# Softmax stage of a two-layer decoder: the twelve output matmuls of a unit stand together, behind the transposes

## The chip, the cores and the metric

The kernel runs on one core of a Trainium2 chip. The metric is the device time of one execution in microseconds (us). The engines of the core work side by side, each through a queue of its own in order, and wait for each other by semaphores: TensorE (PE, with its weight loads as PEld), VectorE (DVE), ScalarE (ACT), GpSimd (POOL) and SyncE (SP), which issues the loads and stores.

## What is computed

Two layers over 2048 positions of width 1024: first sliding-window attention with a sink per head, then a pooling mixer. The change lies in the attention. Cut to what matters:

```python
scores = jnp.einsum('bnqkgd,bnskd->bnkgqs', qb, kb) * (HEAD_DIM ** -0.5)     # 16 blocks of 128 queries
scores = jnp.where(mask, scores, -jnp.inf)                                    # own block and the one before
m = jnp.maximum(jnp.max(scores, axis=-1, keepdims=True), sink)
p = jnp.exp(scores - m)
denom = jnp.sum(p, axis=-1, keepdims=True) + jnp.exp(sink - m)
o = jnp.einsum('bnkgqs,bnskd->bnqkgd', p / denom, vb)                         # 4 key heads, 16 query heads
x = x + gate * ((o * jax.nn.silu(g)) @ w_out)
```

## The kernel before

Four stages follow each other: `qkv_stage`, `gate_stage`, `attend_stage` (the softmax stage) and `pool_layer`. Results between them go through device memory. Products of float32 are made of three matmuls, high x high, high x low and low x high, so that most data exist as a high and a low part.

`attend_stage` works through 64 units (`UNITS`), one for each block of 128 queries and each key head with its four query heads. Sixteen units (`LAP`) make a block of 512 positions. All engines run the same loop over i, each with its own part of several units, so that the steps of one unit are spread over four iterations. In iteration i stand:

- TensorE: `scores(i)`, eight matmuls of 256 columns (L1232); `p_round(i-1)`, four transposes of the probabilities `pr` into the PSUM tile `tr` (L1240), which wait for `prob_done` of unit i-1; `values(i-2)`, twelve matmuls of 256 columns into `o_ps` (L1256), which wait for the masked probabilities `pt`.
- VectorE: `gated(i-3)`, which multiplies `o_ps` by the gate into `z` (L1168) and waits for `values(i-3)`, done by TensorE in iteration i-1; `divide(i-1)`, a reciprocal (L1152) and a multiply of `pr` (L1154) that gives `prob_done`; `scores(i)`, a predicated copy (L1144) and a maximum (L1148); `z_lo(i-3)` (L1175), the low part of `z`; `residual(c)` in the iteration in which chunk c has ended (L1183); `p_lo(i-1)` (L1160), the low part of the transposed probabilities.
- ScalarE: `z_hi(i-3)`, `previous(i)` (L1091), `p_hi(i-1)` (L1106), which waits for the transposes, the four exponentials of `exps(i)` (L1099), and `square(c)` (L1123).
- GpSimd: four masks, two of the high part `ph` and two of the low part `pl` (L1051), and `add_square(c)` (L1060), one addition of two tiles in SBUF for each chunk but the first of eight.

The output projection of a block of 512 positions (`output`, L1270) is 8 chunks (c) of 128 output channels, each 24 matmuls of 512 columns. The chunks of the first three blocks (c = 0 to 23) are spread over the units of the next block: chunk c begins in iteration `first_slot(c)` and takes two iterations, twelve matmuls in each. That is iterations 19 to 66. The last eight chunks follow behind the loop. A chunk ended before iteration i has its `residual`, `square` and `add_square` in iteration i; these are the odd iterations from 21 on, and the addition on GpSimd falls into the end of the odd iteration or the start of the even one. The order on each queue is the order in which the code is written. The loop of TensorE is the only place that the change touches (L1284 to L1303, the functions as they are called there).

Of the kernel before, what the change touches and what calls it, by code (L numbers as in the profile page):

```python
# [23 lines left out]
def wait(eng, sem, count):  # L24
    if not (isinstance(count, int) and count <= 0):
        eng.wait_ge(sem, count)
# [870 lines left out]
def attend_stage(nc, sems, others, xt_d, sinks_d, qt_d, kt_d, vs_d, sg_d, wo_d, x1t_d, ident, gate0, rstd1, KC, NB, KV, HEADS, HD, D):  # L897
# [13 lines left out]
    with ExitStack() as ctx:  # L911
# [42 lines left out]
        def first_slot(c):  # L954
            return LAP * (c // KC + 1) + BEHIND + HALVES * (c % KC)
# [7 lines left out]
        def place(m):  # L963
            cur, prev = m % 3, (m - 1) % 3
            return min(cur, prev), max(cur, prev), 0 if cur < prev else 1

        with nc.Block() as block:
# [251 lines left out]
            @block.tensor  # L1219
            def _(pe):  # L1220
                def scores(u):
                    m, g = u // KV, u % KV
                    low, high, _ = place(m)
                    if g == 0:
                        pe.wait_ge(q_loaded[m % 2], 16 * (m // 2 + 1))
                        pe.wait_ge(k_loaded[m % 3], 16 * (m // 3 + 1))
                        if m == 0:
                            pe.wait_ge(zero_set, 1)
                    wait(pe, cur_done, u - 1)
                    for h in range(GROUP):  # L1230
                        for part in (HI, LO):
                            last = nc.tensor.matmul(s_ps[:, u % 2, h, :, :], qt[:, m % 2, GROUP * g + h, :],  # L1232
                                                    kt[:, low:high + 1:high - low, g, part, :], start=(part == HI), stop=(part == LO))
                    last.then_inc(s_done, 1)

                def p_round(u):
                    pe.wait_ge(prob_done, u + 1)
                    wait(pe, pl_done, u)
                    for h in range(GROUP):
                        last = nc.tensor.transpose(tr[:, h * P:(h + 1) * P], pr[:, u % 2, h, 0:P], ident[:, :])  # L1240
                    last.then_inc(ptr_done, 1)

                def values(u):
                    m, g = u // KV, u % KV
                    if g == 0:
                        pe.wait_ge(v_loaded[m % 3], 16 * (m // 3 + 1))
                    pe.wait_ge(pt_done, 4 * (u + 1))
                    wait(pe, z_done, u)
                    parts = [(m % 3, (CUR_HI, CUR_LO))] + ([((m - 1) % 3, (PREV_HI, PREV_LO))] if m > 0 else [])
                    i = 0  # L1250
                    for slot, kinds in parts:
                        for v_part, p_part in PRODUCTS:
                            moving = pt[:, u % 2, kinds[p_part], :].rearrange("p (a b t) -> p a b t", a=2, b=2)
                            for parity in (0, 1):
                                v = vs[:, slot, g, v_part, HD - parity * HD:HD - parity * HD + 2 * HD]
                                last = nc.tensor.matmul(o_ps[:, 0:2 * P], v, moving[:, :, parity, :],  # L1256
                                                        start=(i == 0), stop=(i == 6 * len(parts) - 1))
                                i += 1
                    last.then_inc(o_done, 1)

                def output(c, ks):
                    s, d = c // KC, c % KC
                    if ks[0] == 0:
                        pe.wait_ge(w_loaded[c % 3], 16 * (c // 3 + 1))
                        wait(pe, x1_done, c - 1)
                    if d == 0:
                        pe.wait_ge(zlo_done, LAP * (s + 1))
                    for k in ks:
                        for a, b in PRODUCTS:
                            last = nc.tensor.matmul(y_ps[:, c % 2, :], w[:, c % 3, a, k, :], zt[:, s % 2, b, k, :],  # L1270
                                                    start=(k == 0 and (a, b) == PRODUCTS[0]),
                                                    stop=(k == KC - 1 and (a, b) == PRODUCTS[-1]))
                    if ks[-1] == KC - 1:
                        last.then_inc(y_done, 1)

                def sum_squares(s):
                    pe.wait_ge(acc_done, (KC - 1) * (s + 1))
                    wait(pe, mq_done, s)
                    pe.wait_ge(z_done, min(LAP * (s + 2) + 2, UNITS))
                    for t in range(PER):  # L1280
                        last = nc.tensor.matmul(o_ps[:, 2 * P + t:2 * P + t + 1], acc[:, t * P:(t + 1) * P], ones[:, :], start=True, stop=True)
                    last.then_inc(st_done, 1)

                pe.wait_ge(consts_set, 5)  # L1284
                quarter = KC // HALVES // 2
                for i in range(LAST):
                    part = [(c, (i - first_slot(c)) * 2 * quarter) for c in range(CHUNKS - KC) if 0 <= i - first_slot(c) < HALVES]
                    if i < UNITS:
                        scores(i)
                    for c, k in part:  # L1290
                        output(c, list(range(k, k + quarter)))
                    if 1 <= i <= UNITS:
                        p_round(i - 1)
                    for c, k in part:
                        output(c, list(range(k + quarter, k + 2 * quarter)))
                    s = (i - BEHIND - 1) // LAP - 2
                    if i == LAP * (s + 2) + BEHIND + 1 and s >= 0:
                        sum_squares(s)
                    if 2 <= i <= UNITS + 1:
                        values(i - 2)  # L1300
                for c in range(CHUNKS - KC, CHUNKS):
                    output(c, list(range(KC)))
                    if c == CHUNKS - KC:  # L1303
                        sum_squares(NSB - 2)
                sum_squares(NSB - 1)
# [415 lines left out]
```

## Time and profile before

| | us |
|---|---|
| median of three runs | 1749.41 (1747.71 to 1750.42) |
| the profiled execution | 1747.5 |
| its span | 1745.8 |
| TensorE busy | 1524.6 (87%) |
| VectorE busy | 861.6 (49%) |
| ScalarE busy | 549.7 (31%) |
| GpSimd busy | 391.0 (22%) |
| output matmuls in the softmax stage, L1270 | 198.6 for 768, 400 ns each |

The softmax stage runs from about 770 to 1175 us of the span. The end of a matmul is modelled, so the start of one block to the start of the next tells more than the busy time. In the timeline a row is a group of instructions that follow each other: its start, its length, engine, line, operation, output and inputs, count, and in brackets how long the engine was idle before it and what released it.

### The profile page before, as it was taken

What the parts mean: (1) busy time and instruction counts of PE and PEld (TensorE: products, weight loads), DVE (VectorE), ACT (ScalarE), POOL (GpSimd) and SP (SyncE); (2) the same over time, 40 slices, a digit from 0 to 9 for tenths busy, and PEclk for the clock granted to TensorE, in tenths of its full rate; (3) what the DMA queues carried; (4) which work ended last, traced back from release to release, by engine and by line L of the source; (5) the groups of instructions that cost most, each with busy time, mean ns of one, the idle gap of its engine ahead of it and who ended that gap; (6) DMA issues with size and microseconds to landing.
All of it is one profiled execution on the core that took longest, in us unless ns stands there. A gap on an engine that the chain in (4) does not pass through costs nothing. (4 is left out here: it accounts for less than half of the span.)

```text
span 1745.8 us, 20594 instructions
## 1 busy us (share of the span) xinstructions
PE 1524.6 (87%) x7466; PEld 1290.1 (74%) x7466; DVE 861.6 (49%) x1509; ACT 549.7 (31%) x1274; POOL 391.0 (22%) x559
## 2 busy tenths in 40 slices
PE   8857787977876899947999999973999999999999
PEld 8746666766665788837888888862888788888787
DVE  1444555345543344438777777415355644345621
ACT  1332323223223122127665655303122222122210
POOL 1032312323111332227655555320000000000000
PEclk9978888888887999979999999986999999999999
DMA  5434442443439877675567766454111255111132
GB/s 197 155 126 165 149 141 112 157 163 124 154 146 356 309 293 299 223 279 198 181 260 278 271 262 255 166 174 141 49 49 49 72 167 193 50 49 49 55 127 97
DMA packets 96709, 294.04 MB, mean 168 GB/s; under 512 B 10816, under 2 KB 35424, under 8 KB 85856
## 3 DMA queue, kind: packets, MB, share of 16 engines
q1 hardware_dynamic: 88320, 262.28, 42.2%
q0 software_dynamic: 8288, 30.44, 4.7%
q8 instruction: 60, 0.98, 0.2%
q14 instruction: 41, 0.34, 0.1%
HBM read 200.41 MB, written 92.27 MB: 168 GB/s over the span
## 5 line engine op out<-in xcount | busy, mean ns | idle before, releaser
L1632 PE MATMUL po_f_ps<-po_ht,po_w 128*128 128x512 f32 x1536 | 351.7, 391 | 28.5 <-DVE po_ht L1535 28.5
L563 PE MATMUL qk_proj<-qk_w_qkv,qk_ht 128*128 128x512 f32 x1152 | 311.8, 432 | 60.4 <-DVE qk_ht L394 58.9
L1632 PEld LDWEIGHTS po_f_ps<-po_ht,po_w 128*128 128x128 f32 x1536 | 290.2, 189 | 89.7 <-issue 18.8
L563 PEld LDWEIGHTS qk_proj<-qk_w_qkv,qk_ht 128*128 128x128 f32 x1152 | 239.0, 212 | 116.4 <-DVE qk_ht L394 60.8
L1270 PE MATMUL at_y_ps<-at_zt,at_w 128*128 128x512 f32 x768 | 198.6, 400 | 4.4 <-DMA at_w<-out_weight_split 4.3
L860 PE MATMUL ga_g_ps<-ga_ht,ga_w_g 128*128 128x512 f32 x768 | 180.5, 394 | 20.4 <-DMA ga_ht<-ht_split 20.4
L860 PEld LDWEIGHTS ga_g_ps<-ga_ht,ga_w_g 128*128 128x128 f32 x768 | 144.3, 190 | 50.4 <-DMA ga_ht<-ht_split 20.8
L1646 PE MATMUL po_y_ps<-po_zt,po_w 128*128 128x512 f32 x768 | 176.9, 392 | 5.2 <-DVE po_zt L1560 5.2
L1646 PEld LDWEIGHTS po_y_ps<-po_zt,po_w 128*128 128x128 f32 x768 | 145.2, 189 | 36.2 <-DVE po_zt L1560 6.0
L1270 PEld LDWEIGHTS at_y_ps<-at_zt,at_w 128*128 128x128 f32 x768 | 138.6, 190 | 30.3 <-DMA at_w<-out_weight_split 5.7
L256 POOL TENSOR_TENSOR qk_rq<-qk_mq,qk_half 128x8 f32<-128x8 f32 (+1 forms) x48 | 70.1, 1461 | 322.8 <-DVE qk_mq L412 322.8
L1504 DVE TENSOR_TENSOR po_w<-po_raw,po_w 128x1024 fp32r<-128x1024 f32 x48 | 58.8, 1226 | 129.3 <-ACT po_w L1439 129.3
L1051 POOL TENSOR_SCALAR_AFFINE_SELECT at_pt<-at_ph 128x512 fp32r<-128x512 f32 x128 | 83.4, 674 | 151.2 <-ACT at_ph L1106 151.2
L409 DVE TENSOR_REDUCE qk_sq<-qk_squares 128x8 f32<-128x512 f32 (+1 forms) x48 | 28.6, 596 | 163.0 <-ACT qk_squares L302 163.0
L1256 PE MATMUL at_o_ps<-at_pt,at_vs 128*128 128x256 f32 x744 | 101.8, 285 | 0.0
L1099 ACT ACTIVATE at_pr<-at_sc,at_neg_max 128x129 f32<-128x129 f32 x256 | 99.7, 393 | 4.6 <-DVE at_neg_max L1148 2.3
L1256 PEld LDWEIGHTS at_o_ps<-at_pt,at_vs 128*128 128x128 f32 x744 | 96.9, 190 | 4.9
L1232 PE MATMUL at_s_ps<-at_kt,at_qt 128*128 128x256 f32 x512 | 75.1, 292 | 18.9 <-DMA at_kt<-keys_t 18.9
L1051 POOL TENSOR_SCALAR_AFFINE_SELECT at_pt<-at_pl 128x512 fp32r<-128x512 f32 x128 | 86.4, 698 | 1.3 <-DVE at_pl L1160 0.2
L1439 ACT ACTIVATE po_w<-po_raw 128x1024 fp32r<-128x1024 f32 x48 | 50.6, 1055 | 112.9 <-PE po_y_ps L1646 112.5
L1232 PEld LDWEIGHTS at_s_ps<-at_kt,at_qt 128*128 128x128 f32 x512 | 69.1, 200 | 18.9 <-issue 18.9
L1567 DVE SCALAR_TENSOR_TENSOR po_x<-po_y_ps,mod,po_x 128x512 f32<-128x512 f32 x32 | 24.0, 751 | 104.0 <-PE po_y_ps L1646 104.0
(152 smaller groups left out, 1808.2 us busy)
## 6 DMA issues: line engine op xcount, KB each, us to landing
at_w<-out_weight_split SPq DMA_DIRECT2D x32, 1024.0 KB, 6.7
ht_split<-qk_ht SPq DMA_DIRECT2D x8, 2048.0 KB, 9.4
queries_t<-qk_late SPq DMA_DIRECT2D x16, 1024.0 KB, 3.8
ga_ht<-ht_split SPq DMA_DIRECT2D x4, 4096.0 KB, 19.8
ga_ada<-in_ada_w POOLq DMA_DIRECT2D x64, 256.0 KB, 6.2
at_qt<-queries_t SPq DMA_DIRECT2D x16, 1024.0 KB, 8.2
values_split<-qk_late SPq DMA_DIRECT2D x16, 768.0 KB, 5.2
at_vs<-values_split SPq DMA_DIRECT2D x16, 768.0 KB, 5.2
```

Source lines behind the costliest of these rows:

```text
L256: nc.gpsimd.tensor_tensor(rq[:, heads], mq[:, heads], half[:, heads], ALU.pow).then_inc(rq_done, 1)
L563: last = nc.tensor.matmul(proj[:, b * BANK:(b + 1) * BANK], ht[:, s % 2, m, k, t * P:(t + 1) * P], w_qkv[:, w, k, b * BANK:(b + 1) * BANK] ...
L860: last = nc.tensor.matmul(g_ps[:, q % 4, :], w_g[:, w, f, k * P:(k + 1) * P], ht[:, s % 2, m, k, :], start=(i == 0), stop=(i == 3 * KC - 1))
L1051: nc.gpsimd.affine_select(out=pt[:, u % 2, kind, :].rearrange("p (h t) -> p h t", h=GROUP), in_=(ph if hi else pl)[:, :].rearrange("p (h t ...
L1099: last = nc.scalar.activation(pr[:, u % 2, h, :], sc[:, g, h, :], ACT.Exp, bias=neg_max[:, u % 2, h:h + 1], accum_out=den[:, u % 2, h:h + 1])
L1232: last = nc.tensor.matmul(s_ps[:, u % 2, h, :, :], qt[:, m % 2, GROUP * g + h, :], kt[:, low:high + 1:high - low, g, part, :], start=(part ...
L1256: last = nc.tensor.matmul(o_ps[:, 0:2 * P], v, moving[:, :, parity, :], start=(i == 0), stop=(i == 6 * len(parts) - 1))
L1270: last = nc.tensor.matmul(y_ps[:, c % 2, :], w[:, c % 3, a, k, :], zt[:, s % 2, b, k, :], start=(k == 0 and (a, b) == PRODUCTS[0]), stop=( ...
L1439: nc.scalar.activation(w[:, i % 2, HI].rearrange("p k c -> p (k c)"), raw[:, i % 3].rearrange("p k c -> p (k c)"), ACT.Copy).then_inc(w_hi, 1)
L1504: nc.vector.tensor_tensor(w[:, i % 2, LO].rearrange("p k c -> p (k c)"), raw[:, i % 3].rearrange("p k c -> p (k c)"), w[:, i % 2, HI].rear ...
L1632: last = nc.tensor.matmul(f_ps[:, bank(j, h), :], w[:, i % 2, a, k, :], ht[:, h, m, k, :], start=(n == 0), stop=(n == 3 * KC - 1))
L1646: last = nc.tensor.matmul(y_ps[:, h, :], w[:, i % 2, a, k, :], zt[:, h, m, k, :], start=(n == 0), stop=(n == 3 * KC - 1))
```

## The change

In TensorE's loop the call of `output` in two halves of six matmuls, one ahead of `p_round(i-1)` and one behind it, becomes one call of twelve matmuls behind `p_round(i-1)`. Nothing else differs.

```diff
                     if i < UNITS:
                         scores(i)
-                    for c, k in part:
-                        output(c, list(range(k, k + quarter)))
                     if 1 <= i <= UNITS:
                         p_round(i - 1)
                     for c, k in part:
-                        output(c, list(range(k + quarter, k + 2 * quarter)))
+                        output(c, list(range(k, k + 2 * quarter)))
```

The order on TensorE before, two iterations from the middle of the first block of output units; `at_s_ps` are the scores, `at_y_ps` the output, `at_tr` the transposed probabilities, `at_o_ps` the values:

```order
L1232 MATMUL at_s_ps<-at_kt,at_qt 128x256 x8
L1270 MATMUL at_y_ps<-at_zt,at_w 128x512 x6
L1240 MATMUL at_tr<-ident,at_pr 128x128 x4
L1270 MATMUL at_y_ps<-at_zt,at_w 128x512 x6
L1256 MATMUL at_o_ps<-at_pt,at_vs 128x256 x12
L1232 MATMUL at_s_ps<-at_kt,at_qt 128x256 x8
L1270 MATMUL at_y_ps<-at_zt,at_w 128x512 x6
L1240 MATMUL at_tr<-ident,at_pr 128x128 x4
L1270 MATMUL at_y_ps<-at_zt,at_w 128x512 x6
L1256 MATMUL at_o_ps<-at_pt,at_vs 128x256 x12
```

The order on TensorE after, two iterations at the same place:

```order
L1232 MATMUL at_s_ps<-at_kt,at_qt 128x256 x8
L1240 MATMUL at_tr<-ident,at_pr 128x128 x4
L1270 MATMUL at_y_ps<-at_zt,at_w 128x512 x12
L1256 MATMUL at_o_ps<-at_pt,at_vs 128x256 x12
L1232 MATMUL at_s_ps<-at_kt,at_qt 128x256 x8
L1240 MATMUL at_tr<-ident,at_pr 128x128 x4
L1270 MATMUL at_y_ps<-at_zt,at_w 128x512 x12
L1256 MATMUL at_o_ps<-at_pt,at_vs 128x256 x12
```

The transposes now follow the scores directly, and the six output matmuls that stood between them stand with the other six. On VectorE, at the same place, an even and an odd iteration, which read the same before and after; the transposes wait for the multiply (`at_pr`), which stands behind the gating (`at_z`):

```order
L1168 SCALAR_TENSOR_TENSOR at_z<-at_o_ps,at_sg 128x256
L1152 RECIPROCAL at_rden<-at_den 128x4
L1154 TENSOR_TENSOR at_pr<-at_pr,at_rden 128x4x128
L1144 COPY_PREDICATED at_sc<-at_keep_cur,at_s_ps 128x4x128
L1148 TENSOR_REDUCE at_neg_max<-at_sc 128x4
L1175 TENSOR_TENSOR at_zt<-at_z,at_zt 128x2x128
L1183 SCALAR_TENSOR_TENSOR at_x<-at_y_ps,gate,at_x 128x512
L1160 TENSOR_TENSOR at_pl<-at_tr,at_ph 128x512
```

Nothing moved there. The row of L1183 stands in odd iterations only.

## Rows read from the trace of the kernel before

**Rows 1.** Busy us by stretch (x instructions), granted clock, DMA share, GB/s.

```profile
core 0: us, PE busy (x) PEld busy (x) DVE busy (x) ACT busy (x) POOL busy (x), PEclk, DMA share, GB/s
805.00:848.00 43.00, 33.47 (x257) 30.39 (x256) 37.90 (x76) 32.42 (x118) 33.17 (x43) 1.00 0.47 170
849.95:939.00 89.05, 89.05 (x567) 78.77 (x566) 66.57 (x118) 54.54 (x184) 47.63 (x71) 1.00 0.66 240
```

**Rows 2.** Timeline of TensorE: even unit from 933.64, odd unit from 939.38.

```profile
933.64 1.11 PE L1232 MATMUL at_s_ps<-at_kt,at_qt 128*128 128x256 f32 x8
...
936.05 0.42 PEld L1240 LDWEIGHTS at_tr<-ident,at_pr 128*128 128x128 f32 x4 [0.34 <-DVE at_pr L1154]
...
936.46 1.64 PE L1270 MATMUL at_y_ps<-at_zt,at_w 128*128 128x512 f32 x6
...
939.38 1.12 PE L1232 MATMUL at_s_ps<-at_kt,at_qt 128*128 128x256 f32 x8
940.33 1.56 PE L1270 MATMUL at_y_ps<-at_zt,at_w 128*128 128x512 f32 x6
941.72 0.60 PE L1240 MATMUL at_tr<-ident,at_pr 128*128 128x128 f32 x4
942.08 1.64 PE L1270 MATMUL at_y_ps<-at_zt,at_w 128*128 128x512 f32 x6
943.55 1.60 PE L1256 MATMUL at_o_ps<-at_pt,at_vs 128*128 128x256 f32 x12
944.99 1.11 PE L1232 MATMUL at_s_ps<-at_kt,at_qt 128*128 128x256 f32 x8
```

**Rows 3.** Timeline of VectorE and GpSimd over the same two units.

```profile
934.15 1.30 POOL L1060 TENSOR_TENSOR at_acc<-at_acc,at_sqx 128x512 f32<-128x512 f32 x1
...
934.38 1.62 DVE L1154 TENSOR_TENSOR at_pr<-at_pr,at_rden 128x512 f32<-128x512 f32 x1
...
937.41 1.38 POOL L1051 TENSOR_SCALAR_AFFINE_SELECT at_pt<-at_ph 128x512 fp32r<-128x512 f32 x2 [1.97 <-ACT at_ph L1106]
...
939.58 0.42 DVE L1168 SCALAR_TENSOR_TENSOR at_z<-at_o_ps,at_sg 128x256 f32<-128x256 f32 x1 [1.26 <-PE at_o_ps L1256]
...
940.12 0.69 DVE L1154 TENSOR_TENSOR at_pr<-at_pr,at_rden 128x512 f32<-128x512 f32 x1
...
942.55 0.42 DVE L1175 TENSOR_TENSOR at_zt<-at_z,at_zt 128x256 fp32r<-128x256 f32 x1
...
943.02 1.22 POOL L1051 TENSOR_SCALAR_AFFINE_SELECT at_pt<-at_ph 128x512 fp32r<-128x512 f32 x2 [3.06 <-ACT at_ph L1106]
...
943.54 0.68 DVE L1160 TENSOR_TENSOR at_pl<-at_tr,at_ph 128x512 f32<-128x512 f32 x1
...
944.30 1.22 POOL L1051 TENSOR_SCALAR_AFFINE_SELECT at_pt<-at_pl 128x512 fp32r<-128x512 f32 x2
...
945.49 1.29 POOL L1060 TENSOR_TENSOR at_acc<-at_acc,at_sqx 128x512 f32<-128x512 f32 x1
```

**Rows 4.** Timeline, iteration 19, the first unit with output matmuls.

```profile
848.99 1.12 PE L1232 MATMUL at_s_ps<-at_kt,at_qt 128*128 128x256 f32 x8
...
850.21 0.69 DVE L1154 TENSOR_TENSOR at_pr<-at_pr,at_rden 128x512 f32<-128x512 f32 x1
...
854.60 1.11 PE L1232 MATMUL at_s_ps<-at_kt,at_qt 128*128 128x256 f32 x8
```

**Rows 5.** Timeline of TensorE, iteration 65, which has no transposes.

```profile
1110.77 2.89 PE L1270 MATMUL at_y_ps<-at_zt,at_w 128*128 128x512 f32 x12
1113.50 1.60 PE L1256 MATMUL at_o_ps<-at_pt,at_vs 128*128 128x256 f32 x12
```

**Rows 6.** Timeline of GpSimd: first and last addition beside units, 19 in all.

```profile
877.52 1.29 POOL L1060 TENSOR_TENSOR at_acc<-at_acc,at_sqx 128x512 f32<-128x512 f32 x1
...
1105.57 1.29 POOL L1060 TENSOR_TENSOR at_acc<-at_acc,at_sqx 128x512 f32<-128x512 f32 x1
```

**Rows 7.** What output matmuls waited for: us in total, times.

```profile
  DMA at_w<-out_weight_split: 10.0, 5
```

## The prediction, made before the changed kernel ran

> **What bounds the kernel now.** I read three views. First the busy time by stretch [rows 1], to see which engine fills the stage: in the 89.05 us from 849.95 on, the stretch in which units carry output matmuls, TensorE is busy for all 89.05 us at a granted clock of 1.00, with VectorE at 66.57 us. Before that, without output matmuls, it is busy 33.47 of 43.00 us. So from iteration 19 of the loop on TensorE sets the pace, and a wait put on its queue there is time added to the kernel. Then the timeline of TensorE over two units [rows 2], to see how long a unit is and what is left between the blocks. I call an iteration of the loop a unit and count from the start of its score matmuls. The even unit at 933.64 is 5.74 us long (to 939.38), the odd one at 939.38 is 5.61 us (to 944.99). Last the timeline of VectorE and GpSimd over the same two units [rows 3], to see when the probabilities, for which the transposes wait, are written.
>
> What matters is the order in VectorE's queue: gated, reciprocal, multiply, then the rest. In iteration i, gated(i-3) waits for the values matmuls that TensorE did at the end of iteration i-1, and the multiply of divide(i-1), which p_round(i-1) waits for, stands behind it. So in every unit the transposes can't start before values of the unit before + gated + reciprocal + multiply. In the odd unit: gated starts at +0.20 (939.58), the multiply at +0.74 (940.12) and it ends at +1.43 (940.12 + 0.69) [rows 3]; the first transpose follows 0.05 us behind such an end (even unit: 934.38 + 1.62 = 936.00, transpose at 936.05), so at +1.48 at the earliest. The score matmuls are over at +0.95 (940.33) [rows 2]. Today the six output matmuls, 1.39 us (940.33 to 941.72), lie over that gap: the transposes are due at +2.34 and need the data at +1.48. **Those six matmuls are the cover that the change takes away.** Nothing but the scores lies ahead of the transposes afterwards.
>
> **The change part by part.** It adds and removes no instruction; on SP, GpSimd, ScalarE and VectorE every queue keeps its order, and no DMA is moved.
>
> Twelve in a row. A block of twelve that follows values and is followed by values takes 2.73 us (1110.77 to 1113.50) [rows 5]. Six behind transposes take 1.47 us (942.08 to 943.55) against 1.39 us behind scores [rows 2], so I put 0.08 us on it: 2.81 us, where the two blocks now take 1.39 + 1.47 = 2.86 us. That is the whole of the direct gain, 0.05 us a unit. The transposes take 0.41 us to the next block when they had to wait (936.05 to 936.46) and values 1.44 us (943.55 to 944.99) [rows 2].
>
> Units without disturbance. 1.48 + 0.41 + 2.81 + 1.44 = 6.14 us against 5.61: +0.53 us.
>
> Units with GpSimd's add. add_square(c) reads two tiles of SBUF, as the multiply does. In the even unit the add runs from 934.15 to 935.45 and the multiply, issued at 934.38, takes 1.62 us in place of 0.69, ending 0.55 us behind the add [rows 3]. The first and last adds beside units are at 877.52 and 1105.57 [rows 6]; there are 19, one in each even unit from 24 to 64 but 38 and 54, since the first chunk of a block of eight needs none. In the odd unit the add starts 6.11 us behind the unit's start (939.38 to 945.49), held by p_lo (943.54) and the two masks of 1.22 us behind it (944.30) [rows 3]. That chain hangs on VectorE's gated and ScalarE's copy of the scores, not on the transposes, so it keeps its place from the unit's start. Since the odd unit is now 6.14 us, the add would begin at -0.03 of the even unit.
>
> One thing moves it. The masks of the high part start 1.36 us behind a transpose that had to wait (936.05 to 937.41) [rows 2, 3]: in the new odd unit at +2.84, where today it is +3.64 (943.02). z_lo, which also reads two tiles of SBUF, runs from +3.17 (942.55, 0.42 us); today it is ahead of the masks, afterwards behind their start. That the two meet is seen in the even unit, where a mask pair issued 0.12 us behind z_lo takes 1.38 us and not 1.22 [rows 3]. Bounds for z_lo: not held, it ends at +3.59; held to the end of the first mask (2.84 + 0.61 = 3.45), it ends some 0.28 us behind that, at +3.73; held over both masks, at +4.34. I take the middle one, +0.14 us, as the pair's row shows only one lock being waited out. residual, p_lo, the masks of the low part and the add stand behind z_lo and move as much: the add at +0.11 to +1.40 of the even unit, the multiply ending at 1.40 + 0.55 = +1.95, the transposes at +2.00, the unit 2.00 + 0.41 + 2.81 + 1.44 = 6.66 us against 5.74: +0.92 us. With z_lo not held: 6.52 us, +0.78. Held over both: the add from +0.72 to +2.01, just ahead of the multiply, and 7.27 us, +1.53.
>
> Does the add hold gated too? gated now falls beside it (+0.20, add from +0.11). It reads PSUM and one tile of SBUF, and no row shows such an instruction issued during an add. Lower bound nothing. Upper bound: gated ends 0.28 us behind the add (+1.68), the multiply runs from +1.80 to +2.49, the unit is 2.54 + 0.41 + 2.81 + 1.44 = 7.20 us, +1.46. I take nothing, since the reads in the rows that were stretched were pairs from SBUF. The Trainium skill ("SBUF — State Buffer", section "SBUF: two separate sides") says that only a VectorE instruction in a 2-port mode or with two SBUF inputs contends with GpSimd, and that the one that starts first keeps the shared pair for its whole length while the other is fully blocked. By that rule gated goes free and the sum stays; the multiply's row agrees in kind, with 1.62 us against 0.69.
>
> The first unit, iteration 19. There the chain of softmax is the later one, since the stretch before is not bound by TensorE: the multiply ends at 850.21 + 0.69 = 850.90, the unit starts at 848.99 [rows 4]. Transposes at +1.96, the unit 6.62 us against 5.61 (848.99 to 854.60): +1.0 us.
>
> Iterations 65 and 66 have no transposes and are as before; sum_squares keeps its place.
>
> **Sum.** Units 20 to 64 are 45: 19 x 0.92 = 17.5 us and 26 x 0.53 = 13.8 us; with the first, 17.5 + 13.8 + 1.0 = 32.3 us. The profiled execution took 1747.5 us, which gives 1779.8; the median of the runs is 1749.4, 1.9 us above it, and the same 32.3 us give **1781.7 us**. Nothing behind the stage gives it back: the last eight chunks and the pool layer follow in series.
>
> **The rivals.**
> - The add comes clear of the multiply (GpSimd does it before the unit begins, or behind the multiply). For it: the forecast has it begin within 0.11 us of the unit's start, and small shifts decide. Against: 1.29 us long [rows 3], it would have to begin 0.55 us sooner. Even units then take 6.14 us, +0.40: 19 x 0.40 + 13.8 + 1.0 = 22.4 us, 1771.8 us. Chance 0.08.
> - The loads of the last chunks give some back. Output matmuls now wait 10.0 us in all, five times, for the out weights [rows 7], all in the tail. If the slower loop put those loads ahead, up to 10 us come back: 1771.7 us. Against: each load waits for the matmuls of an earlier chunk and so stays as close to them. Chance 0.05.
> - More contention: z_lo held over both masks gives 19 x 1.53 + 14.8 = 43.9 us, 1793.3 us; gated held gives 19 x 1.46 + 14.8 = 42.5 us, 1791.9 us. Chance 0.12 together.
> - The other side, a gain. If the probabilities were ready at +0.90, the transposes would not wait, and a unit would take 0.95 + 0.36 + 2.81 + 1.44 = 5.56 us: 19 x 0.18 + 26 x 0.05 = 4.7 us less, 1744.7 us. It decides at one point, the multiply's end in the odd unit at +1.43 [rows 3]. For it speaks only that the loop as a whole has slack (VectorE 66.57 of 89.05 us [rows 1]); against it, that gated stands ahead of the multiply in a queue that runs in order, and the slack is elsewhere. Chance 0.04. The Trainium skill ("Perfetto Trace Analysis", section "Matmul Optimizations") says that matmuls should run back to back in batches as the engine scales its power with use; here the granted clock is 1.00 already, so that adds nothing to the gain.
> - The change moves the code but the time stays within 0.2%, because another wait that I hold to be free ends as late today. TensorE shows none in the stretch [rows 1]. Chance 0.03.
> - TensorE's clock falls from 2.4 to 1.2 GHz in the new gaps of 0.5 to 1 us. Against: from 805 to 848 it is idle for 9.53 of 43.00 us and is granted 1.00 [rows 1]. If a tenth of the 46 units ran at half speed it would cost 4.6 x 5.56 = 26 us more, 1807 us. Chance 0.03.
>
> **How the numbers follow.** The forecast, with z_lo held once or not (1781.7 or 19 x 0.78 + 14.8 = 29.6 us, 1779.0), has 0.65. Range 1770 to 1794: from the two lower cases to the two with more contention; outside lie the gain, no change, the clock, and a little of each side, 0.1 to 0.15 in all. A measurement of this kernel can tell 0.2%, 3.5 us, from no change. Slower by more: 0.65 + 0.08 + 0.05 + 0.12 + 0.03 = 0.93; within: 0.03; faster: 0.04.
>
> **What would show it.** Right: TensorE idle before the transposes, released by the multiply, in all 46 units with output matmuls and transposes; odd units of 6.1 us; even units of 6.6 us with the multiply at 1.2 to 1.5 us; twelve output matmuls in 2.8 us; the stretch of output units longer by 32 us and nothing else changed. Wrong: transposes that start at +0.95 without a wait, units of one length (the add clear of the multiply), gated longer than 0.42 us, or a granted clock below 1.00.

## The result, and the profile after

The changed kernel takes 1781.98 us in the median of four runs (1781.19 to 1787.14) against 1749.70 us; the ratio is 1.0193, 95% interval 1.0171 to 1.0214. It is slower by 32 us, where 32.3 us were forecast. In the three later sets of runs, those of the experiments, the kernel before came to 1747.6 to 1747.9 us in the median (13 to 23 runs each), so the loss is 32 to 34 us. That the loss is real is clear of the interval; whether it is more or less than 2% is not.

The profiled execution of after is the longest of the four, 1787.14 us with a span of 1785.4, 39.6 us above the span before. Its parts show what of that belongs to the change: 3.6 us lie ahead of the softmax stage, where nothing differs (its first score matmuls start at 773.69 against 770.07), 1.7 us in the units ahead of iteration 19, which have no output matmuls, and 34.4 us in the units from iteration 19 to 64 (854.31 to 1150.47, 296.16 us, against 848.99 to 1110.77, 261.78 us). All that follows takes 634.9 us, as before (635.0). The 1.7 us are a difference between executions: that stretch takes 78.9 us in E6 below, which has the changed order on TensorE, and 80.6 us in E9, which has the old one.

The busy time by stretch (us, instructions in brackets, granted clock, share of the DMA engines, GB/s) in the output units after, where [rows 1] had TensorE busy without a gap:

```profile
861.00:950.00 89.00, 81.15 (x506) 71.38 (x506) 58.29 (x105) 49.45 (x161) 42.53 (x61) 1.00 0.58 216
```

TensorE is now idle for 7.85 of 89.00 us, at the same granted clock of 1.00. What it waits for, by the view of the transposes' line (us in total, times, for weight loads and matmuls together):

```profile
L1240 PE MATMUL at_tr<-ident,at_pr x256: 272/273/477, 780.7 to 1146.1; 128*128 128x128 f32 x128
its engine sat idle before it (us, times) until:
  DVE at_pr L1154: 111.5, 128
```

128 waits are all 64 groups of transposes, each counted once as load and once as matmul: not one starts without a wait for VectorE's multiply. (For the kernel before the same view has 53.5 us, 56 times.) The timeline over an odd unit (from 930.92) and the even one behind it (from 937.10), to be laid beside [rows 2, 3]:

```profile
930.92 1.11 PE L1232 MATMUL at_s_ps<-at_kt,at_qt 128*128 128x256 f32 x8
931.12 0.42 DVE L1168 SCALAR_TENSOR_TENSOR at_z<-at_o_ps,at_sg 128x256 f32<-128x256 f32 x1 [2.62 <-PE at_o_ps L1256]
...
931.66 0.69 DVE L1154 TENSOR_TENSOR at_pr<-at_pr,at_rden 128x512 f32<-128x512 f32 x1
...
932.40 0.66 PE L1240 MATMUL at_tr<-ident,at_pr 128*128 128x128 f32 x4 [0.38 <-DVE at_pr L1154]
...
932.82 3.00 PE L1270 MATMUL at_y_ps<-at_zt,at_w 128*128 128x512 f32 x12
...
933.77 1.40 POOL L1051 TENSOR_SCALAR_AFFINE_SELECT at_pt<-at_ph 128x512 fp32r<-128x512 f32 x2 [3.62 <-ACT at_ph L1106]
934.09 0.59 DVE L1175 TENSOR_TENSOR at_zt<-at_z,at_zt 128x256 fp32r<-128x256 f32 x1
...
935.65 1.60 PE L1256 MATMUL at_o_ps<-at_pt,at_vs 128*128 128x256 f32 x12
...
937.10 1.11 PE L1232 MATMUL at_s_ps<-at_kt,at_qt 128*128 128x256 f32 x8
937.19 1.28 POOL L1060 TENSOR_TENSOR at_acc<-at_acc,at_sqx 128x512 f32<-128x512 f32 x1
937.30 0.42 DVE L1168 SCALAR_TENSOR_TENSOR at_z<-at_o_ps,at_sg 128x256 f32<-128x256 f32 x1 [1.36 <-PE at_o_ps L1256]
...
937.84 1.19 DVE L1154 TENSOR_TENSOR at_pr<-at_pr,at_rden 128x512 f32<-128x512 f32 x1
...
939.08 0.66 PE L1240 MATMUL at_tr<-ident,at_pr 128*128 128x128 f32 x4 [0.88 <-DVE at_pr L1154]
...
943.78 1.11 PE L1232 MATMUL at_s_ps<-at_kt,at_qt 128*128 128x256 f32 x8
```

The transposes start at +1.48 of the odd unit and at +1.98 of the even one, each 0.05 us behind the end of the multiply. The odd unit is 6.18 us long, the even one 6.68 us.

Unit lengths from here on are those of the regular units. Left out, unless named, are iteration 19, iterations 36 and 52, in which TensorE also does `sum_squares` (6.61 us before, 7.55 and 7.58 us after), and iteration 64, which has no scores.

### The profile page after: what moved, and what is told of

The parts are those of the page before. It is cut to its first block and busy times, and to the rows that moved or that the text cites. A ratio compares the mean times of both kernels' runs of the same rounds, so it can differ in the third digit from the quotient of the medians.

```text
span 1785.4 us, 20594 instructions
## 1 busy us (share of the span) xinstructions
PE 1537.2 (86%) x7466; PEld 1299.3 (73%) x7466; DVE 859.9 (48%) x1509; ACT 553.3 (31%) x1274; POOL 395.7 (22%) x559
## 5 line engine op out<-in xcount | busy, mean ns | idle before, releaser
L1270 PE MATMUL at_y_ps<-at_zt,at_w 128*128 128x512 f32 x768 | 189.9, 399 | 5.1 <-DMA at_w<-out_weight_split 5.1
L1051 POOL TENSOR_SCALAR_AFFINE_SELECT at_pt<-at_ph 128x512 fp32r<-128x512 f32 x128 | 88.1, 711 | 162.2 <-ACT at_ph L1106 162.2
L1240 PE MATMUL at_tr<-ident,at_pr 128*128 128x128 f32 x256 | 43.4, 294 | 49.1 <-DVE at_pr L1154 49.1
```

What stands on the lines that cost most here:

```text
L1051: nc.gpsimd.affine_select(out=pt[:, u % 2, kind, :].rearrange("p (h t) -> p h t", h=GROUP), in_=(ph if hi else pl)[:, :].rearrange("p (h t ...
```

## The experiments

Each kernel is the one named with the edit shown. Its time stands beside runs of the kernel before in the same set and on the same chip (1747.6 to 1747.9 us in the median), and the ratio is to these.

**E1, the swap on VectorE in the changed kernel.** Is it the order gated, then multiply, that makes TensorE wait?

```diff
+                    early = LAP + BEHIND < i <= UNITS
+                    if early:
+                        divide(i - 1)
                     if 0 <= i - BEHIND < UNITS:
                         gated(i - BEHIND)
-                    if 1 <= i <= UNITS:
+                    if 1 <= i <= UNITS and not early:
                         divide(i - 1)
```

> The changed kernel with one swap on VectorE: in iterations 20 to 64 divide(i-1) stands ahead of gated(i-3). Theory (the transposes wait because their multiply stands behind gated, which waits for values of the iteration before): the exponentials end about +4.95 us into a unit, so the multiply is done near the start of the next one, the transposes start at +0.95 without a wait and the unit is 0.95 + 0.36 + 2.83 + 1.44 = 5.58 us, odd and even. With the first unit still 1 us longer: 1745 to 1749 us. Rival (the new form itself is slow: transposes directly behind scores, or twelve output matmuls in a row): nothing changes, 1782 us. Rival (GpSimd's add holds the multiply whatever stands ahead of it): odd units 5.6, even units still 6.1 or more, 1757 us or above.

Measured 1756.9 us, ratio 1.0059 (1.0039 to 1.0078). Some 25 of 34 us come back, which sets aside the rival that the form of the blocks costs; but 8 to 12 us more than expected are left. The units are 5.6 us at first and then 5.76 (odd) and 5.84 us (even), and the multiply, which now falls beside GpSimd's masks, takes 1.05 to 1.12 us in place of 0.69. The timeline of one turn in E1, an odd unit from 935.74:

```profile
935.70 1.05 DVE L1154 TENSOR_TENSOR at_pr<-at_pr,at_rden 128x512 f32<-128x512 f32 x1
935.74 1.11 PE L1235 MATMUL at_s_ps<-at_kt,at_qt 128*128 128x256 f32 x8
936.68 0.41 DVE L1168 SCALAR_TENSOR_TENSOR at_z<-at_o_ps,at_sg 128x256 f32<-128x256 f32 x1
936.81 0.66 PE L1243 MATMUL at_tr<-ident,at_pr 128*128 128x128 f32 x4
937.12 0.42 ACT L1113 ACTIVATE at_zt<-at_z 128x256 fp32r<-128x256 f32 x1 [1.67 <-DVE at_z L1168]
...
937.45 0.58 ACT L1091 ACTIVATE at_sc<-at_s_ps 128x512 f32<-128x512 f32 x1
...
938.06 0.75 DVE L1144 COPY_PREDICATED at_sc<-at_keep_cur,at_s_ps 128x512 f32<-128x512 uint32 x1 [0.97 <-ACT at_sc L1091]
...
941.47 1.12 DVE L1154 TENSOR_TENSOR at_pr<-at_pr,at_rden 128x512 f32<-128x512 f32 x1
```

`previous` (L1091) starts 1.71 us into the unit and not 1.15, because it stands behind `z_hi` (L1113) on ScalarE, which waits for gated, which now waits for the multiply. That closes a ring from multiply to multiply: 935.70 + 1.05 = 936.75 to 941.47 + 1.12 = 942.59, 5.84 us. My expectation had overlooked ScalarE's queue.

**E5, the swap with `z_hi` out of the ring.** On ScalarE `z_hi(i-3)` goes behind `p_hi(i-1)`:

```diff
-                    if 0 <= i - BEHIND < UNITS:
+                    early = LAP + BEHIND < i <= UNITS
+                    if 0 <= i - BEHIND < UNITS and not early:
                         z_hi(i - BEHIND)
                     if i < UNITS:
                         previous(i)
                     if 1 <= i <= UNITS:
                         p_hi(i - 1)
+                    if early:
+                        z_hi(i - BEHIND)
```

> The changed kernel with divide(i-1) ahead of gated(i-3) on VectorE, and z_hi(i-3) behind p_hi(i-1) on ScalarE, both in iterations 20 to 64. New theory for the 5.8 us units of the swap alone: the swap put gated behind the multiply, z_hi waits for gated, and previous(i) stands behind z_hi on ScalarE, so a ring multiply, gated, z_hi, previous, copy, maximum, exponentials, reciprocal, multiply was closed, and with a multiply held by the masks (1.05 to 1.12 us) it is 5.8 us long. With z_hi out of the way previous(i) starts at +1.15, the exponentials end near +4.95 and the multiply is done before the next unit's +0.95: units of 5.58 us, 1744 to 1749 us. Rival (the masks hold the multiply past +0.95 whatever the ring does): units stay at 5.75 or above, 1755 us.

Measured 1745.5 us, ratio 0.9990 (0.9978 to 1.0003). The loss is gone, within what the runs can tell, with the output matmuls still in one block of twelve behind the transposes. The timeline of an odd unit of E5, from 942.14, and the mask pair and multiply ahead of it:

```profile
941.12 1.23 POOL L1051 TENSOR_SCALAR_AFFINE_SELECT at_pt<-at_pl 128x512 fp32r<-128x512 f32 x2 [0.94 <-DVE at_pl L1163]
...
941.74 1.15 DVE L1157 TENSOR_TENSOR at_pr<-at_pr,at_rden 128x512 f32<-128x512 f32 x1
942.14 1.11 PE L1238 MATMUL at_s_ps<-at_kt,at_qt 128*128 128x256 f32 x8
...
943.09 0.60 PE L1246 MATMUL at_tr<-ident,at_pr 128*128 128x128 f32 x4
943.29 0.60 ACT L1091 ACTIVATE at_sc<-at_s_ps 128x512 f32<-128x512 f32 x1 [1.80 <-PE at_s_ps L1238]
```

The masks still hold the multiply (1.15 us), but it ends at +0.75 and the transposes start at +0.95 with no wait. Units are 5.58 to 5.61 us, but for iteration 19, which the swap does not reach (6.64 us), and 37 and 53 (5.9 us). The rival that the masks alone set 5.8 us falls.

**E6, the control for E5:** `z_hi` late, VectorE as in the changed kernel.

> The changed kernel with z_hi(i-3) behind p_hi(i-1) on ScalarE alone, gated still ahead of divide. Theory: previous(i) waits for the scores until +1.15 and z_hi is over at +1.07, so nothing moves: odd units 6.18, even 6.68 us, 1782 us within 3 us. Rival (ScalarE's place of z_hi was the cost, not VectorE's order): back towards 1750 us.

Measured 1782.1 us, ratio 1.0194 (1.0176 to 1.0211), with odd units of 6.16 to 6.18 and even ones of 6.67 to 6.72 us: ScalarE's order does nothing by itself. **E2, the control for E1:** the swap on VectorE in the kernel before.

> The kernel before with the same swap on VectorE. Theory: its transposes wait only in the even units, about 0.12 us each, 19 times, so at most 2.3 us go: 1747 to 1750 us, no more than 0.2% from the kernel before. The rival that the swap speeds the loop by itself, whatever the place of the output matmuls, would give a gain like that of the swap in the changed kernel, some 30 us, 1718 us.

Measured 1745.5 us, ratio 0.9989 (0.9976 to 1.0001). All its units are 5.59 to 5.62 us, so the 0.12 us in even units are gone, as expected. So the swap is worth some 25 us where the cover is missing and about 2 us where it stands; the interval of the second holds no change as well, and the unit lengths are the better evidence for it.

**E3, the whole cover:** all twelve output matmuls ahead of the transposes.

```diff
-                    if 1 <= i <= UNITS:
-                        p_round(i - 1)
                     for c, k in part:
                         output(c, list(range(k, k + 2 * quarter)))
+                    if 1 <= i <= UNITS:
+                        p_round(i - 1)
```

> All twelve output matmuls stand ahead of the transposes, none behind: the cover is 2.73 us in place of 1.39. Theory: no transposes wait, odd and even units take 0.95 + 2.78 + 0.36 + 1.44 = 5.53 to 5.58 us, 1744 to 1747 us. A block of twelve is as in the changed kernel, so the rival that twelve in a row are slow gives 1782 us here too. Rival (the transposes come 1.4 us later in the unit, and the chain from them over the masks to values, or to the exponentials, ends late): above 1750 us, with waits on values for the masks.

Measured 1743.1 us, ratio 0.9975 (0.9964 to 0.9987), the lowest median of all, and clear of the kernel before by its interval. Units are 5.56 to 5.59 us. The block of twelve is as long as in the changed kernel; only its side of the transposes differs, and with it 39 us. No wait of values for the masks came up. E3 in the timeline, the unit from 933.52:

```profile
933.52 1.11 PE L1232 MATMUL at_s_ps<-at_kt,at_qt 128*128 128x256 f32 x8
...
934.47 2.91 PE L1270 MATMUL at_y_ps<-at_zt,at_w 128*128 128x512 f32 x12
934.65 0.69 DVE L1154 TENSOR_TENSOR at_pr<-at_pr,at_rden 128x512 f32<-128x512 f32 x1
...
937.23 0.60 PE L1240 MATMUL at_tr<-ident,at_pr 128*128 128x128 f32 x4
937.58 1.67 PE L1256 MATMUL at_o_ps<-at_pt,at_vs 128*128 128x256 f32 x12
...
939.09 1.12 PE L1232 MATMUL at_s_ps<-at_kt,at_qt 128*128 128x256 f32 x8
```

The multiply ends at +1.82 and the transposes come at +3.71: nearly 2 us of cover are unused.

**E7, a quarter of the cover:** three output matmuls ahead, nine behind.

```diff
                     if i < UNITS:
                         scores(i)
+                    for c, k in part:
+                        output(c, [k])
                     if 1 <= i <= UNITS:
                         p_round(i - 1)
                     for c, k in part:
-                        output(c, list(range(k, k + 2 * quarter)))
+                        output(c, list(range(k + 1, k + 2 * quarter)))
```

> Three of the twelve output matmuls ahead of the transposes, nine behind. They cover 0.70 us, to +1.65. Theory: the odd units need +1.48, so their wait is gone and they are 5.6 us. For the even units the add then begins at about +0.75 of them, at the same moment at which the multiply is issued (+0.74): if the add is first, the multiply ends near +2.55, the transposes start at +2.60 and the even units with an add are 6.5 us, 1765 us in all; if the multiply is first they are 5.6 us, 1748 us. Rival (only the form of the blocks counts, and any output matmuls behind the transposes cost in proportion): 12 behind cost 34 us and 6 behind nothing, so 9 behind some 17 us, spread evenly over odd and even units (both about 5.95 us).

Measured 1745.5 us, ratio 0.9987 (0.9975 to 0.9999); units are 5.60 to 5.62 us, odd and even; only iteration 19, where the multiply is later, is longer, with 5.95 us. The rival of a cost in proportion falls (17 us were its forecast): 0.70 us of cover are enough. Of the two outcomes left open it was the one in which the multiply is first, in all 19 units with an add. An even unit of E7, from 934.34:

```profile
934.34 1.11 PE L1232 MATMUL at_s_ps<-at_kt,at_qt 128*128 128x256 f32 x8
...
935.08 0.69 DVE L1154 TENSOR_TENSOR at_pr<-at_pr,at_rden 128x512 f32<-128x512 f32 x1
935.12 1.80 POOL L1060 TENSOR_TENSOR at_acc<-at_acc,at_sqx 128x512 f32<-128x512 f32 x1
935.29 0.86 PE L1270 MATMUL at_y_ps<-at_zt,at_w 128*128 128x512 f32 x3
...
935.99 0.60 PE L1240 MATMUL at_tr<-ident,at_pr 128*128 128x128 f32 x4
```

The multiply starts 0.04 us ahead of the add and takes its plain 0.69 us; the add takes 1.80 us in place of 1.29. Which of the two is held turns on a few hundredths of a microsecond, so that 0.70 us is enough in these units by a narrow margin: by the expectation, an add that came first would have left 6.5 us.

**E4, no add:** GpSimd's addition is cut to one column, which leaves out most of the sum of squares.

```diff
-                        nc.gpsimd.tensor_tensor(acc[:, :], acc[:, :], sqx[:, c % 2], ALU.add).then_inc(acc_done, 1)
+                        nc.gpsimd.tensor_tensor(acc[:, 0:1], acc[:, 0:1], sqx[:, c % 2, 0:1], ALU.add).then_inc(acc_done, 1)
```

> The changed kernel with GpSimd's add cut to one column, so the sum of squares leaves out most of itself. Theory: the multiply of the even units no longer waits, 0.69 in place of 1.19 us, and the even unit falls from 6.68 to 6.18 us: 19 x 0.50 = 9.5 us, 1772.5 us; the odd units stay at 6.18 us with their wait of about 0.5 us. Rival (the whole loss comes from the add): back to 1750 us.

Measured 1771.9 us, ratio 1.0141 (1.0117 to 1.0165). Odd and even units are 6.16 to 6.20 us (37 and 53: 6.26), as expected: the add costs 0.50 us in each of 19 units, 9.5 to 10 us, and the rest of the loss, 24 us, is the wait for the multiply behind gated. An even unit of E4, from 934.95, in which the multiply takes its plain 0.69 us:

```profile
934.95 1.11 PE L1232 MATMUL at_s_ps<-at_kt,at_qt 128*128 128x256 f32 x8
935.05 0.19 POOL L1060 TENSOR_TENSOR at_acc<-at_acc,at_sqx 128x1 f32<-128x1 f32 x1
...
935.69 0.69 DVE L1154 TENSOR_TENSOR at_pr<-at_pr,at_rden 128x512 f32<-128x512 f32 x1
...
936.44 0.65 PE L1240 MATMUL at_tr<-ident,at_pr 128*128 128x128 f32 x4 [0.38 <-DVE at_pr L1154]
```

**E8 and E9, gated twice,** the first time into a spare tile, in the changed kernel and in the one before, for the units gated in iterations 20 to 64.

```diff
+                    if LAP < u <= UNITS - BEHIND:
+                        nc.vector.scalar_tensor_tensor(spare[:, u % 2], o_ps[:, 0:2 * P].rearrange("p (a t) -> p a t", a=2), 0.5,
+                                                       sg[:, m % 2, 2 * g:2 * g + 2, :], ALU.mult, ALU.mult)
```

> The changed kernel with the gating done twice in iterations 20 to 64, the first time into a spare tile, so that 0.34 to 0.42 us more stand ahead of the multiply on VectorE. Theory: the units without an add wait for the gating and grow by all of it, 6.18 to 6.54 us, 26 x 0.36 = 9.4 us. The even units with an add wait for the add (it ends at +1.37), not for the gating: the add begins some 0.36 us sooner in them as the odd units are longer, the multiply is issued at +1.10 and ends at +1.79, the transposes start at +1.84 in place of +1.98, so they go from 6.68 to 6.54 us, 19 x -0.14 = -2.7 us. Together 6.7 us: 1789 us. Rival (gating and add are both in a row on the path): 45 x 0.36 = 16 us, 1798 us. Rival (VectorE's order is not what TensorE waits for): 1782 us.

Measured 1793.0 us, ratio 1.0263 (1.0244 to 1.0281), 11 us above the changed kernel. The odd units grew from 6.18 to 6.52 us, by what was put in, and the even units with an add stayed at 6.68, where 6.54 was expected. In one of them, from 936.57:

```profile
936.67 1.29 POOL L1061 TENSOR_TENSOR at_acc<-at_acc,at_sqx 128x512 f32<-128x512 f32 x1
...
937.64 0.86 DVE L1155 TENSOR_TENSOR at_pr<-at_pr,at_rden 128x512 f32<-128x512 f32 x1
```

The multiply is issued at +1.07 and ends 0.54 us behind the add, so it is the add that sets this unit. What I had missed is that the add moves with the odd unit: masks and `z_lo` shift there too, and it begins at +0.10 again. So the two waits are not in a row: the longer one counts. 26 x 0.35 = 9.1 us for the units without an add and nothing for the others lie near the 11 us of the medians and the 9 us of the table below, and the rival's 16 us do not.

> The kernel before with the same second gating. Theory: its odd units need the probabilities at +1.48 + 0.36 = +1.84 and have cover to +2.34; in the even units the multiply is still held to the end of the add at +1.80. No unit grows: the kernel before within 0.2%, 1748 us. Rival (the gating costs its own time wherever the output matmuls stand): 16 us more, 1764 us.

Measured 1748.0 us, ratio 1.0007 (0.9996 to 1.0019). The odd units stay at 5.61 us, so there the longer chain is covered. The even units with an add went from 5.73 to 5.86 us, which I had not expected: in one of them (from 936.88) the add starts at +0.63 and no longer at +0.51, and the multiply ends behind it. The odd unit ahead shows why: with more gating on VectorE, its `z_lo` starts at +3.31 in place of +3.17, and what stands behind that, the add last, moves with it.

```profile
936.88 1.11 PE L1236 MATMUL at_s_ps<-at_kt,at_qt 128*128 128x256 f32 x8
...
937.51 1.29 POOL L1061 TENSOR_TENSOR at_acc<-at_acc,at_sqx 128x512 f32<-128x512 f32 x1
...
937.95 1.40 DVE L1155 TENSOR_TENSOR at_pr<-at_pr,at_rden 128x512 f32<-128x512 f32 x1
```

The medians scatter by a microsecond or two; the length of iterations 19 to 64 in the profiled execution can be read more finely:

| Kernel | median of its runs, us | iterations 19 to 64, us |
|---|---|---|
| before | 1747.6 to 1749.7 | 261.8 |
| changed | 1782.0 | 296.2 |
| E1, swap | 1756.9 | 269.4 |
| E5, swap, `z_hi` late | 1745.5 | 260.6 |
| E6, `z_hi` late alone | 1782.1 | 296.2 |
| E2, swap, in the kernel before | 1745.5 | 258.8 |
| E3, twelve ahead | 1743.1 | 257.4 |
| E7, three ahead | 1745.5 | 259.9 |
| E4, no add | 1771.9 | 286.6 |
| E8, gated twice | 1793.0 | 305.0 |
| E9, gated twice, in the kernel before | 1748.0 | 264.6 |

## Why the prediction was right

Taken step by step, in the order in which it argued:

- **The cover.** It said that the transposes can start at +1.48 and have only the scores ahead of them, to +0.95. The trace of after has +1.48 (930.92 to 932.40). E1 with E5, E3 and E7 show it as the cause: the loss goes when the multiply comes sooner, or when any output matmuls, even three, stand ahead of the transposes.
- **Twelve in a row** were put at 2.81 us and take 2.83 (932.82 to 935.65), so that 0.03 us of the direct gain of 0.05 are there in this unit. In E3, where nothing waits, units are 5.57 us against 5.61.
- **Units without an add:** +0.53 forecast, +0.57 measured (6.18 against 5.61). The 0.04 us are 0.02 in the block of twelve and 0.01 each in transposes and values. 26 x 0.04 = 1.0 us.
- **Units with an add:** +0.92 forecast, +0.94 to 0.95 measured (6.68). The add begins at +0.09 where +0.11 was said, and ends at +1.37; the multiply ends 0.56 us behind it, at +1.93.
- **`z_lo` behind the masks.** The middle value was taken, an end at +3.73; it is +3.76 (934.09 + 0.59), 0.59 us long in place of 0.42. So it waits out one mask, not two.
- **gated beside the add.** Nothing was taken, 1.46 us a unit was the upper bound. It is issued 0.11 us behind the add's start (937.30 against 937.19) and takes 0.42 us. By the rule in the Trainium skill ("SBUF — State Buffer", section "SBUF: two separate sides") a VectorE instruction with two inputs from SBUF is blocked by a GpSimd instruction that reads SBUF and came first, and one with a single SBUF input, outside a 2-port mode, is not; the traces agree, with 0.42 us for gated, and 1.19 in place of 0.69 for the multiply. The trace of before could have said it for another instruction: `p_lo`, with one input in PSUM and one in SBUF, runs beside the masks at 937.41 [rows 3] and is not stretched.

```profile
937.63 0.68 DVE L1160 TENSOR_TENSOR at_pl<-at_tr,at_ph 128x512 f32<-128x512 f32 x1
```

- **The first unit:** 6.62 us forecast, 6.63 measured (854.31 to 860.94).
- **Missed, and small:** iterations 37 and 53, where VectorE computes the mean of squares ahead of gated. There the unit went from 5.60 to 6.27 us, 0.1 us more than the others.
- **Read too strongly:** that TensorE shows no wait in the stretch before the change. The even units with an add had one, the 0.34 us of the transposes' load in [rows 2], and that is why they were 0.12 us longer. E2 takes these 0.12 us away, 19 times. The sum was not touched, as it counts the even units from their 5.74 us.

Sum by the profile: 34.4 us for 32.3, 2.1 us under; the medians give 32 to 34 us. The mechanism held step by step, but that the median came within 0.3 us of the 1781.7 us forecast is in part luck: the 1749.4 us it was added to lie 2 us above the later medians of the kernel before, and that made up for a sum 2 us too small. Of the rivals, the add did not come clear of the multiply, the loads of the last chunks gave nothing back (output matmuls waited 10.0 us for them before [rows 7] and 11.4 us after), and the granted clock stayed at 1.00 through idle gaps of 0.4 to 0.9 us a unit. For the last chunks, the view of the output's line after:

```profile
L1270 PE MATMUL at_y_ps<-at_zt,at_w x768: 387/389/796, 856.7 to 1209.1; 128*128 128x512 f32 x192
...
  DMA at_w<-out_weight_split: 11.4, 6
```

## What to carry to other kernels

An engine that is busy all the time can still owe it to where its independent work stands: before a block is moved, look up at what moment the next waiting instruction's data are ready, counted from what the unit's other engines wait for, and leave at least that much work ahead of the wait. Here 0.7 us of the 2.8 us of output matmuls did for it, in the units with an add by a few hundredths of a microsecond, and with none the unit lost 0.6 to 0.9 us. When a step is put first on one queue, follow all that then stands behind it, on the next engines too; E1 closed a new ring in that way.

## What the runs showed of the hardware

- In these traces a VectorE multiply of two SBUF tiles and a GpSimd addition of two SBUF tiles hold each other in both directions, by who starts first. Issued 0.22 to 0.98 us into the add, the multiply takes until 0.54 to 0.56 us behind the add's end (before, after, E6, E8, E9); started 0.04 us ahead of the add it takes its plain 0.69 us and the add 1.80 us in place of 1.29 (E7). In either order the one held ends about 0.14 us sooner than if it had begun only at the other's end.
- A VectorE instruction with two SBUF inputs that is issued during the first of a pair of masks gets its turn between them: `z_lo` took 0.59 us in place of 0.42 and ended 0.3 us behind the first of the two (after, 934.09), not behind the second.
